# Output projection and MLP of a hybrid residual layer: seven-product first MLP layer, one block for output and MLP stages, token tiles in paired order

## The chip, the cores and the metric

One Trainium2 chip, one core. The metric is device time in microseconds (us) of the whole kernel, and the median of three runs is compared. TensorE is written PE, VectorE DVE, ScalarE ACT, GpSimd POOL, and the engine that issues the DMAs SP.

## What is computed

One layer of a streaming encoder over 1024 tokens of width 1024, all float32. What matters here are its last two lines; `mix` comes from a time mixer (RWKV-7 and stick-breaking attention), whose stages the change doesn't touch.

```
mix = merged @ w_out                                   # 1024x1024 @ 1024x1024
x   = layernorm(ALPHA * x + g1 * mix, ln1_g, ln1_b)
h   = modulate(x, sh2, sc2)                            # a second normalization, then scale and shift
ff  = square(relu(h @ w_ff1 + b_ff1)) @ w_ff2 + b_ff2  # 1024 -> 4096 -> 1024
out = layernorm(ALPHA * x + g2 * ff, ln2_g, ln2_b)
```

Each float32 matrix product is made of three bf16 products. An operand is split into a high part (its bf16 rounding, a copy on ACT) and a low part (what is left, a subtraction on POOL), and PE forms high*high + high*low + low*high.

## The kernel before

The program is a row of phases, each a block in which all five engines run their own queue of instructions in order and meet at a barrier at its end. The last three are `phase_merge` (which also begins the output product of the first token tile), `phase_out` and `phase_mlp`.

**`phase_out`** takes the 8 token tiles of 128 tokens in order. For tile t PE makes 48 matmuls of 512 columns (`out_products`, L2015). DVE adds the residual (L2346) and takes statistics; ACT normalizes (L2294); DVE applies gain (L2353) and bias (L2355), takes statistics again, ACT normalizes again into `ou_yn` (semaphore `n2`, L2282). PE transposes it (`turned_tile`, L2383) in the middle of tile t + 2, ACT scales and shifts it into `ou_hf` and copies the high part to `a_hi` (L2275), POOL makes `a_lo` (L2247). `keep` (L2335) writes the new residual to `g.x1`, a part of the buffer `z`. While the last tile is finished, PE works on the first two of the 32 tiles of 128 hidden columns (`ff_part`, L2206), with token columns that are ready.

**`phase_mlp`** takes the 32 hidden tiles in 8 groups of 4 (`GT`). `group` makes the first layer of 4 hidden tiles, 48 matmuls of 512 columns each (`gemm_rows`, L218), with ReLU on ACT (L2515), square on DVE (L2607), high part on ACT (L2519) and low part on POOL (L2552). `second` multiplies a finished group with its rows of `w_ff2` in 16 blocks of 12 matmuls (L674), which DVE adds to `g.x1` (L2619). PE makes `group(i + 1)` before `second(i)`. The weights of the first layer are loaded per hidden tile (512 KB) and split on ACT (L2437) and POOL (L2441); those of the second are loaded per group (2 MB), scaled by g2 on DVE (L2599) and split on ACT (L2524) and POOL (L2557). The last group is followed by the last normalization.

The functions that the diff touches:

Of the kernel before, what the change touches and what calls it, by code (L numbers as in the profile page):

```python
# [7 lines left out]
F32 = mybir.dt.float32  # L8
# [2201 lines left out]
def phase_out(nc, g, a):  # L2210

    with ExitStack() as es:
        sb = lambda n, s=(P, D), d=F32: es.enter_context(nc.sbuf_tensor(f"ou_{n}", list(s), d))
        names = "vec brow mm y s1 v1 sd1 r1 n1 gain bias keep s2 v2 sd2 r2 n2 turn hf hi lo tail_hf tail_hi".split()
        per_tile = {"mm": 2, "y": 2, "s1": 2, "s2": 2, "r1": 2, "r2": 2, "hf": KT}
        s = {n: nc.alloc_semaphore(f"ous_{n}") for n in names}
        s_x = [nc.alloc_semaphore(f"ous_x{u}") for u in range(2)]
        xt, y, yn = ([sb(f"{n}{u}") for u in range(2)] for n in ("x", "y", "yn"))
        hf = sb("hf", (P, KT, P))
        vec = sb("vec", (P, 3, D))  # L2220
# [23 lines left out]
        def low(eng, t):
            if inside(t):
                wait(eng, t, "hi")
                eng.tensor_tensor(g.a_lo[:, :, tok(t)], hf[:], g.a_hi[:, :, tok(t)], ALU.subtract).then_inc(s["lo"], 1)  # L2247
# [477 lines left out]
```

## Time and profile before

| | |
|---|---|
| time, median of 3 runs | 1732.8 us (1730.94 to 1733.28) |
| span of the profiled execution | 1730.9 us |
| output stage, from about 967 us | to 1076 us |
| MLP stage | from 1078 us to the end |
| PE busy | 1643.6 us, 95% of the span |
| DVE, ACT, POOL busy | 769.0, 562.3, 451.3 us |

The time of the profiled execution itself is not listed apart from its span; the median of the three runs is 1.9 us above the span. Times in the rows are in us from the span's start. A matmul of 512 columns is listed with 0.38 us, since its way through the array is counted in, but in a dense run the next one starts 0.216 us later. "[1.95 <-POOLq L88]" behind a row means that the engine was idle for 1.95 us before it, and what ended the wait.

### The profile page before, as it was taken

The numbers are of one execution on the slowest core, as the hardware profiler recorded it, in microseconds if no ns is written. First come the engines' busy times: TensorE is split into PE (matmuls) and PEld (weight loads), VectorE is DVE, ScalarE is ACT, GpSimd is POOL, SyncE is SP. The second block draws the span as 40 slices with busy tenths as digits, with TensorE's granted clock in tenths as the row PEclk, the third lists the DMA queues.
The fourth block names the chain that finished last, engine by engine and source line by source line (L and its number), as shares of the span: only waits on it lengthen the run. The fifth ranks groups of instructions, "written<-read, shape, count | busy, mean of one in ns | idle before, by whom it ended". The sixth has DMA issues, their size and how long they took to land. (4 is left out here: it accounts for less than half of the span.)

```text
span 1730.9 us, 34492 instructions
## 1 busy us (share of the span) xinstructions
PE 1643.6 (95%) x14983; PEld 857.5 (50%) x15178; DVE 769.0 (44%) x1061; ACT 562.3 (32%) x884; POOL 451.3 (26%) x236
## 2 busy tenths in 40 slices
PE   4998999998999998999999999999999999999997
PEld 2444666666545555544444455444444444444443
DVE  5597666666325455313111486433232323232338
ACT  5323544454324555411312165421211212120300
POOL 1231322222110112123422122742323333232310
PEclk9999999999999999999999999999999999999999
DMA  9851001000111200312110311420202021112002
GB/s 354 265 199 41 16 4 39 4 28 28 27 46 28 62 1 1 126 58 61 48 36 25 110 49 47 137 86 25 73 24 73 25 72 36 61 36 85 1 1 97
DMA packets 105773, 109.69 MB, mean 63 GB/s; under 512 B 2592, under 2 KB 82610, under 8 KB 105394
## 3 DMA queue, kind: packets, MB, share of 16 engines
q1 hardware_dynamic: 105648, 107.82, 19.2%
q8 instruction: 103, 1.69, 0.4%
q14 instruction: 22, 0.18, 0.0%
HBM read 101.52 MB, written 4.19 MB: 61 GB/s over the span
## 5 line engine op out<-in xcount | busy, mean ns | idle before, releaser
L218 PE MATMUL tokens_ps<-a_hi,z 128*128 128x512 bf16 x878 | 228.5, 379 | 0.9
L674 PE MATMUL ff_ps<-ff_hi,c_lo 128*128 128x512 bf16 x503 | 190.6, 379 | 0.6
L674 PE MATMUL ff_ps<-ff_hi,c_hi 128*128 128x512 bf16 x501 | 189.9, 379 | 1.4 <-DVE z L2619 0.9
L674 PE MATMUL ff_ps<-ff_lo,c_hi 128*128 128x512 bf16 x501 | 189.9, 379 | 0.6
L2619 DVE TENSOR_TENSOR z<-ff_ps,z 128x512 f32<-128x512 f32 x128 | 88.3, 690 | 205.0 <-PE ff_ps L674 204.3
L2515 ACT ACTIVATE ff_r<-tokens_ps,cols 128x1024 f32<-128x1024 f32 x30 | 33.4, 1114 | 421.4 <-PE tokens_ps L218 414.4
L2441 POOL TENSOR_TENSOR z<-z 128x1024 bf16<-128x1024 f32 x28 | 62.3, 2225 | 345.1 <-ACT z L2437 345.1
L218 PEld LDWEIGHTS tokens_ps<-a_hi,z 128*128 128x128 bf16 x896 | 87.6, 98 | 105.8
L2607 DVE TENSOR_TENSOR ff_r<-ff_r 128x1024 f32<-128x1024 f32 x32 | 41.1, 1284 | 219.2 <-ACT ff_r L2515 219.2
L218 PE MATMUL tokens_ps<-a_lo,z 128*128 128x512 bf16 x438 | 131.1, 379 | 0.5
L195 POOL TENSOR_TENSOR mg_wlo<-mg_stage,mg_whi 128x1024 bf16<-128x1024 f32 x21 | 45.6, 2175 | 149.9 <-ACT mg_whi L191 149.9
L2552 POOL TENSOR_TENSOR c_lo<-ff_r,c_hi 128x1024 bf16<-128x1024 f32 x32 | 75.9, 2371 | 29.4 <-ACT c_hi L2519 29.4
L674 PEld LDWEIGHTS ff_ps<-ff_hi,c_hi 128*128 128x128 bf16 x512 | 50.1, 98 | 61.6 <-issue 1.3
L674 PEld LDWEIGHTS ff_ps<-ff_hi,c_lo 128*128 128x128 bf16 x512 | 50.1, 98 | 60.4
L674 PEld LDWEIGHTS ff_ps<-ff_lo,c_hi 128*128 128x128 bf16 x512 | 50.1, 98 | 60.2
L808 DVE TENSOR_TENSOR_SCAN b_lo<-z,sb_ahead 128x256 f32<-128x256 f32 (+3 forms) x32 | 50.5, 1621 | 46.8 <-ACT z L925 46.8
L218 PEld LDWEIGHTS tokens_ps<-a_lo,z 128*128 128x128 bf16 x448 | 43.8, 98 | 52.9
L2557 POOL TENSOR_TENSOR ff_lo<-ff_st,ff_hi 128x1024 bf16<-128x1024 f32 x32 | 68.1, 2158 | 0.0
L2599 DVE TENSOR_TENSOR ff_st<-ff_st,z 128x1024 f32<-128x1024 f32 x32 | 67.3, 2160 | 1.7 <-DMA ff_st<-w_ff 1.7
L808 DVE TENSOR_TENSOR_SCAN b_hi<-z,sb_ahead 128x128 f32<-128x128 f32 (+3 forms) x32 | 48.3, 1551 | 43.1 <-ACT z L925 43.1
L2169 DVE TENSOR_TENSOR mg_ga<-mg_ga,mg_ps 128x1024 f32<-128x1024 f32 x7 | 8.5, 1221 | 131.6 <-PE mg_ps L218 131.6
L1648 PE MATMUL rw_front<-a_hi,z 128*128 128x512 bf16 x179 | 58.2, 387 | 3.0 <-issue 2.9
(420 smaller groups left out, 3219.2 us busy)
## 6 DMA issues: line engine op xcount, KB each, us to landing
ff_st<-w_ff SPq DMA_DIRECT2D x8, 2048.0 KB, 7.7
z<-w_ff SPq DMA_DIRECT2D x30, 512.0 KB, 4.0
ada_w<-w_ada SPq DMA_DIRECT2D x6, 2048.0 KB, 8.2
z<-w_in SPq DMA_DIRECT2D x18, 512.0 KB, 4.4
z<-w_ada SPq DMA_DIRECT2D x8, 1024.0 KB, 13.5
mg_stage<-w_in SPq DMA_DIRECT2D x16, 512.0 KB, 4.0
zs_stage<-w_in SPq DMA_DIRECT2D x8, 512.0 KB, 8.2
ada_w<-w_ada SPq DMA_DIRECT2D x4, 1024.0 KB, 13.5
```

The costliest lines, as they stand in the source:

```text
L195: pool.tensor_tensor(lo[u][:], stage[u][:], hi[u][:], ALU.subtract).then_inc(lo_ready[u], 1)
L218: last = pe.matmul(out[:, h * HALF:(h + 1) * HALF], w[:, kt, :], a[:, slot, h * HALF:(h + 1) * HALF], start=(x == 0 and y == 0), stop=(x = ...
L674: last = pe.matmul(out, a[:, slot, at], w[:, x, n], start=(x == 0 and y == 0), stop=(x == k - 1 and y == 2))
L808: dve.tensor_tensor_scan(prod[b][:, 0:nk][:, ::-1], m, masked, 1.0, ALU.mult, ALU.max).then_inc(s_scan, 1)
L1648: mm = pe.matmul(unit_bank(u)[:], w_part[:, kt, :], a_part[:, kt, h * HALF:(h + 1) * HALF], start=(x == 0), stop=(x == 3 * KT - 1))
L2441: pool.tensor_tensor(ff.lo[u], stage[u], ff.hi[u], ALU.subtract).then_inc(ff.lo_ready[u], 1)
L2515: act.activation(r[u][:], (wide if begun and t >= begun else ps1)[u][:], ACT.Relu, bias=g.cols[:, ds(gr * GT + (b1 + t), 1)]).then_inc(s_r ...
L2552: pool.tensor_tensor(g.c_lo[:, GT * par + t, :], r[u][:], g.c_hi[:, GT * par + t, :], ALU.subtract).then_inc(s_ulo[u], 1)
L2557: pool.tensor_tensor(lo2[par][:, k, :], st2[:, k, :], hi2[par][:, k, :], ALU.subtract).then_inc(s_o2, 1)
L2599: dve.tensor_tensor(st2[:, k, :], st2[:, k, :], g.g2, ALU.mult).then_inc(s_m2, 1)
L2607: dve.tensor_tensor(r[u][:], r[u][:], r[u][:], ALU.mult).then_inc(s_sq[u], 1)
L2619: dve.tensor_tensor(acc, ps2[x % 4], acc, ALU.add).then_inc(s_acc, 1)
```

## The change

`phase_out` and `phase_mlp` become one function, `phase_tail`, in one block without a barrier between the stages. All its loops are written out.

The first MLP layer takes hidden tiles in pairs (256 hidden columns) and cuts the product of a pair into 2x2 blocks: two halves of the hidden columns, two of the tokens (T0, T1), two of the summed dimension (K0, K1). Instead of eight block products it forms seven, each of 4 x 3 matmuls of 512 columns, out of sums of blocks:

- sums of activation blocks, `sums(i)`: 4 DVE instructions of 512 elements for two token tiles, then 2 high parts on ACT (`sum_high`) and 2 low parts on POOL (`sum_low`). They need a token tile of each half, so the tiles are taken in the order 0, 4, 1, 5, 2, 6, 3, 7 (`ORD`). `sums(0)` stands in the loop's turn 4, `sums(1)` in turn 6, the other two behind the loop.
- sums of weight blocks, `ff_sums`: 4 DVE instructions of 512 elements for a pair, with split copies of 512 + 1024 + 2048 elements on ACT (L2485, L2486, L2490), and as many on POOL (L2594, L2596, L2600).
- sums of products, in `pair`: DVE forms four result quarters and two intermediates (`u2`, `u3`) with 6 instructions of 512 elements that read PSUM; ReLU, square, high and low part are made per quarter (512 elements).

The first two hidden tiles stay plain (`first_part`), so 15 pairs follow, numbered n = 0 to 14. Weight set q = n + 1 is loaded as one transfer of 1 MB into one staging buffer `st1` (so a load waits until the low sums of the set before are made, `s_wsl`); the rows of `w_ff2` come in halves of a group, 1 MB each, into `st2` (a load waits for the low parts of the half before, `s_o2`). The instructions of the last tail of the kernel are the same.

```diff
-            for t in range(TT):
-                wait(pe, t - 2, "y")
-                for h in range(2):
-                    kts = [kt for kt in range(KT) if t or kt not in OUT_AHEAD]
-                    out_products(pe, g, t, slice(h * HALF, (h + 1) * HALF), kts, t > 0, True).then_inc(s["mm"], 1)
-                    if h == 0:
-                        turned_tile(t - 2)
...
+FF_ORDER = (1, 2, 6, 7, 5, 4, 3)
...
+def ff_product(pe, g, w, n, out, onto=False):
+
+    whi, wlo, bhi, blo = ff_operands(g, w)[n]
+    for kt in range(PAIRS):
+        for y, (m, b) in enumerate(((whi, bhi), (whi, blo), (wlo, bhi))):
+            last = pe.matmul(out, m[:, kt, :], b[:, kt, :], start=(kt == 0 and y == 0 and not onto), stop=(kt == PAIRS - 1 and y == 2),
+                             skip_group_check=True)
+    return last
...
+        @block.scalar
...
+                if p == NEXT_AT:
+                    act.wait_ge(s["w1"], 16)
+                    act.activation(set1.d_hi, next_st[:, K1, N1], ACT.Copy).then_inc(s["wah"], 1)
+                    act.activation(set1.a_hi, next_st[:, :, N0], ACT.Copy).then_inc(s["wah"], 1)
+                if p in SUMS_AT:
+                    sum_high(SUMS_AT[p])
+                if p == NEXT_SUMS:
+                    act.wait_ge(s["ws"], 4)
+                    act.activation(set1.s_hi, next_st, ACT.Copy).then_inc(s["wsh"], 1)
...
+            def first():
...
+                act.wait_ge(s_flo, 2)
+                second_high(0, 0, 0)
+                first_high(3, sets[1], True)
+                sums_high(3, sets[1])
+                second_high(0, 0, 1)
...
+        @block.vector
...
+            def pair(n, x, banks, free, after_c11=None, late=None):
+                of = lambda p: quads(bank(banks, x, p))
+                dve.wait_ge(s_p1, n + 1)
+                product(n, 2)
+                free(0)
+                dve.tensor_tensor(quarter(0, 0), u2, of(2), ALU.add).then_inc(s_c, 1)
...
+                product(n, 7)
+                dve.wait_ge(s_c, n * 6 + U2)
+                dve.tensor_tensor(u3, u2, of(7), ALU.add).then_inc(s_c, 1)
+                if late:
+                    late()
+                product(n, 5)
+                dve.wait_ge(s_c, n * 6 + U3)
+                free(1)
+                dve.tensor_tensor(quarter(1, 1), u3, of(5), ALU.add).then_inc(s_c, 1)
...
+            def step(i, par, last, more):
+                gr = i + 1
+                if not last:
+                    freed = lambda n: lambda k: dve.wait_ge(s_ulo, n * 4 + (k - 3))
+                    scale2(gr, 0)
+                    pair(gr * 2 - 1, 0, narrow, freed(gr * 2 - 1))
+                    scale2(gr, 1)
...
+        @block.tensor
...
+            def pair(n, x):
+                w = sets[x]
+                pe.wait_ge(s_wal, n * 2)
...
+                    if p == 5:
+                        pe.wait_ge(s_p1, n + 1)
+                    if p == 4:
+                        pe.wait_ge(s_c, n * 6 + C11)
+                    if p == 3:
+                        pe.wait_ge(s_c, n * 6 + C22)
+                    ff_product(pe, g, w, p, bank(narrow, x, p), p == 3).then_inc(s_prod, 1)
```

What the change does to the order of instructions is shown at three places. The first is ACT's queue in turn 4 of the output loop, from the first normalization of that turn's tile to its second (`yn`). Before:

```order
L2294 ACTIVATE ou_y<-ou_y,ou_rs 128x1024
L2271 ACTIVATE ou_hf<-ou_turned,ada 128x128 x8
L2275 ACTIVATE a_hi<-ou_hf 128x8x128
L150 ACTIVATE c_lo<-c_hi 128x1024
L2286 ACTIVATE ou_rs<-ou_mv,const 128x1
L2282 ACTIVATE ou_yn<-ou_y,ou_rs 128x1024
```

Of the changed kernel, where `tl_wd` and `z` are the high parts of the first weight set and `b_hi` the high parts of the activation sums:

```order
L2460 ACTIVATE tl_y<-tl_y,tl_rs 128x1024
L2430 ACTIVATE tl_pc<-ff_wide,ada 128x128 x8
L2434 ACTIVATE a_hi<-tl_pc 128x8x128
L2452 ACTIVATE tl_rs<-tl_mv,const 128x1
L2467 ACTIVATE tl_wd<-c_hi 128x512
L2468 ACTIVATE z<-c_hi 128x1024
L2439 ACTIVATE b_hi<-tl_pc 128x8x128
L2441 ACTIVATE b_hi<-tl_pc 128x8x128
L2448 ACTIVATE tl_yn<-tl_y,tl_rs 128x1024
```

Four copies now stand between the root (L2452) and the `yn` that PE's transposes wait for; the early copy L150 has moved to turn 1.

The second place is ACT's queue between the last quarter of pair 0 and the copy of pair 1's first product to `u2` (`tl_v`, L2510), in the changed kernel alone. `tl_pc` (L2495) are high parts of `w_ff2`; `tl_wd`, `z` and `tl_wsh` are those of weight set 3:

```order
L2505 ACTIVATE c_hi<-a_hi 128x512
L2495 ACTIVATE tl_pc<-tl_y 128x1024 x2
L2485 ACTIVATE tl_wd<-z 128x512
L2486 ACTIVATE z<-z 128x1024
L2490 ACTIVATE tl_wsh<-z 128x2048
L2495 ACTIVATE tl_pc<-tl_y 128x1024 x2
L2510 ACTIVATE tl_v<-tokens_ps 128x512
```

All the splitting of a weight set stands ahead of the copy that frees pair 1's PSUM bank.

The third place is DVE's queue in the second pair of a group, in the changed kernel alone. L2751 scales rows of `w_ff2`, L2772, L2777, L2781 and L2787 are sums of products, L2259 to L2264 are the sums of the next weight set in the buffer `z`:

```order
L2751 TENSOR_TENSOR tl_y<-tl_y,z 128x1024 x2
L2772 TENSOR_TENSOR a_hi<-tl_v,tokens_ps 128x2x256
L2777 TENSOR_TENSOR tl_v<-tl_v,tokens_ps 128x512
L2762 TENSOR_TENSOR a_hi<-a_hi 128x2x256
L2781 TENSOR_TENSOR tl_v<-tl_v,tokens_ps 128x512
L2259 TENSOR_TENSOR z<-z 128x4x128
L2261 TENSOR_TENSOR z<-z 128x4x128
L2263 TENSOR_TENSOR z<-z 128x4x128
L2264 TENSOR_TENSOR z<-z 128x4x128
L2787 TENSOR_TENSOR a_lo<-tl_v,tokens_ps 128x2x256
```

The weight sums stand in front of the sum (C22) for which PE's product 3 waits.

## Rows read from the trace of the kernel before

**Rows 1.** The page: busy times; shares of the chain that ended last.

```profile
PE 1643.6 (95%) x14983; PEld 857.5 (50%) x15178; DVE 769.0 (44%) x1061; ACT 562.3 (32%) x884; POOL 451.3 (26%) x236
...
PE ff_ps L674 17%; PE tokens_ps L218 17%; PE ff_ps L218 1%; DVE ff_st L2577 1%; DVE z L2594 1%; DVE z L2619 0%; DVE z L2587 0%; DVEq L2452 0%; DVE ff_rs L2589 0%; DVE ff_mv L2581 0%; POOLq L88 0%; DVEq L2593 0%; POOLq L2702 0%
```

**Rows 2.** The chain in order of time: start, us, what.

```profile
1099.66 10.74 PE tokens_ps L218 x49
```

**Rows 3.** Busy time by stretch: length, PE, PEld, DVE, ACT, POOL, PE clock, DMA.

```profile
970.00:1067.00 97.00, 96.53 (x475) 47.90 (x482) 77.96 (x121) 53.37 (x98) 19.06 (x9) 1.00 0.24 79
...
1140.00:1679.00 539.00, 536.22 (x2446) 244.16 (x2495) 157.96 (x161) 102.53 (x101) 167.67 (x76) 1.00 0.14 46
```

**Rows 4.** Timeline of PE at the end of the output stage: start, us, what, wait.

```profile
1073.28 0.23 PE L2206 MATMUL tokens_ps<-a_hi,c_lo 128*128 128x128 bf16 x1 [1.14 <-DVE a_lo L2247]
...
1078.08 0.38 PE L218 MATMUL ff_ps<-a_hi,z 128*128 128x512 bf16 x1 [1.95 <-POOLq L88]
```

**Rows 5.** Timelines of ACT and PE: second normalizations of tiles 4 to 7, transposes of 4 to 6.

```profile
1028.67 1.24 ACT L2282 ACTIVATE ou_yn<-ou_y,ou_rs 128x1024 f32<-128x1024 f32 x1 [1.12 <-DVE ou_rs L2330]
1034.68 1.04 PE L2383 MATMUL ou_turned<-const,ou_yn 128*128 128x128 f32 x8
1039.64 1.24 ACT L2282 ACTIVATE ou_yn<-ou_y,ou_rs 128x1024 f32<-128x1024 f32 x1 [1.72 <-DVE ou_rs L2330]
1045.92 1.04 PE L2383 MATMUL ou_turned<-const,ou_yn 128*128 128x128 f32 x8
1050.72 1.24 ACT L2282 ACTIVATE ou_yn<-ou_y,ou_rs 128x1024 f32<-128x1024 f32 x1 [1.73 <-DVE ou_rs L2330]
1052.02 1.09 PE L2383 MATMUL ou_turned<-const,ou_yn 128*128 128x128 f32 x8
1065.47 1.24 ACT L2282 ACTIVATE ou_yn<-ou_y,ou_rs 128x1024 f32<-128x1024 f32 x1 [1.72 <-DVE ou_rs L2330]
```

**Rows 6.** Timelines of DVE and POOL: one small DVE instruction, twice, and POOL's.

```profile
979.60 0.16 DVE L2330 SCALAR_TENSOR_TENSOR ou_rs<-ou_mv,ou_rs 128x1 f32<-128x1 f32 x1
1055.92 2.12 POOL L2247 TENSOR_TENSOR a_lo<-ou_hf,a_hi 128x1024 bf16<-128x1024 f32 x1 [5.25 <-ACT a_hi L2275]
1056.26 1.80 DVE L2330 SCALAR_TENSOR_TENSOR ou_rs<-ou_mv,ou_rs 128x1 f32<-128x1 f32 x1
```

**Rows 7.** Durations, from timelines and groups of instructions (busy us, mean ns).

```profile
961.21 0.69 DVE L2197 TENSOR_TENSOR mg_m<-mg_ga,mg_gb 128x512 f32<-128x512 f32 x1
961.93 0.63 ACT L2142 ACTIVATE b_hi<-mg_m 128x512 bf16<-128x512 f32 x1 [3.11 <-DVE mg_m L2197]
1204.77 8.50 DVE L2599 TENSOR_TENSOR ff_st<-ff_st,z 128x1024 f32<-128x1024 f32 x4
L2607 DVE TENSOR_TENSOR ff_r<-ff_r 128x1024 f32<-128x1024 f32 x32 | 41.1, 1284 | 219.2 <-ACT ff_r L2515 219.2
L2619 DVE TENSOR_TENSOR z<-ff_ps,z 128x512 f32<-128x512 f32 x128 | 88.3, 690 | 205.0 <-PE ff_ps L674 204.3
L2519 ACT ACTIVATE c_hi<-ff_r 128x1024 bf16<-128x1024 f32 x32 | 33.8, 1057 | 21.1 <-DVE ff_r L2607 21.1
L2247 POOL TENSOR_TENSOR a_lo<-ou_hf,a_hi 128x1024 bf16<-128x1024 f32 x7 | 14.9, 2124 | 89.4 <-ACT a_hi L2275 89.4
```

**Rows 8.** DMA issues: size of each, median us from issue to landing.

```profile
ff_st<-w_ff SPq DMA_DIRECT2D x8, 2048.0 KB, 7.7
z<-w_ff SPq DMA_DIRECT2D x30, 512.0 KB, 4.0
```

**Rows 9.** PE after a wait, and its clock by stretch (length, PE busy, clock).

```profile
678.34 0.63 PE L894 MATMUL tokens_ps<-a_lo,mg_whi 128*128 128x512 bf16 x1 [5.95 <-POOL mg_wlo L154]
...
676.00:677.00 1.00, 0.00 (x0) 0.64 0.00 0
...
682.00:683.00 1.00, 1.00 (x4) 0.50 0.00 0
683.00:684.00 1.00, 1.00 (x6) 0.94 0.00 0
```

More of the change, by code:

```diff
@@ L2207, in ff_part @@
     return last
-def phase_out(nc, g, a):
-    with ExitStack() as es:
[L2213 to L2220, printed above, removed]
+K0, K1 = slice(0, PAIRS), slice(PAIRS, KT)
@@ L2244, in low @@
[L2244 to L2247, printed above, removed]
+        next_st = fl(g.c_hi[:, EARLY_OUT:KT, :]).bitcast(F32).rearrange("p (k n) -> p k n", n=2 * P)
+        names = ("vec brow mm y s1 v1 sd1 r1 n1 gain bias keep s2 v2 sd2 r2 n2 turn hf hi lo "
+                 "sums xhi yhi xlo ylo w1 wah wal ws wsh wsl std").split()
+        per_tile = {"mm": 2, "y": 2, "s1": 2, "s2": 2, "r1": 2, "r2": 2, "hf": KT}
@@ new lines, in phase_tail, with wait @@
+        s_vec, s_st, s_mv, s_sd, s_rs, s_gain, s_bias, s_last, s_out = (
+            sem(n) for n in "vec st mv sd rs gain bias last out".split())
+        block = es.enter_context(nc.Block())
+        inside = lambda p: 0 <= p < TT
+        EARLY_AT, NEXT_AT, NEXT_SUMS = (1, 2), 4, 5
+        SUMS_AT = {4: 0, 6: 1}
+        LOW_AT = {5: 0, 7: 1}
+        def wait(eng, p, name, j=None):
+            k = per_tile.get(name, 1)
+            if p >= 0:
+                eng.wait_ge(s[name], p * k + (k if j is None else j))
@@ L2249, in _, with steps @@
+        def steps(first, step):
+            first()
+            for i in range(NGR):
+                step(i, i % 2, i == NGR - 1, i < NGR - 2)
         @block.sync
@@ new lines, in high, with pair @@
+            def high(par, x, n, k):
+                t, h = QUARTERS[k]
+                act.wait_ge(s_sq, n * 4 + k + 1)
+                act.activation(quads(c_at(g.c_hi, par, x, t, h)), quarter(t, h), ACT.Copy).then_inc(s_uhi, 1)
+            def pair(gr, par, x, n, early=None, late=None):
+                act.wait_ge(s_prod, n * NP + 1)
+                act.wait_ge(s_c, n * 6)
+                act.activation(u2, quads(bank(narrow, x, 1)), ACT.Copy).then_inc(s_p1, 1)
+                for k in range(4):
+                    relu(gr, x, n, k)
+                    if k == 0 and early:
+                        early()
+                    high(par, x, n, k)
+                    if k == 1 and late:
+                        late()
@@ L2572, in _ @@
+            scale(LAST, 1)
+            sums(2)
+            keep(LAST)
+            wait(dve, LAST - 1, "lo")
+            low(dve, LAST)
+            sums(3)
+            sum_low(dve, 3, 1)
             credit(dve, [s_acc])
@@ L2621, in step @@
                         norm(t, h, i * NO + x + 2)
+                    if more and 6 <= x < 10:
+                        weight_sums(gr * 2 + 3, x - 6)
                 if last:
@@ new lines, in first @@
+            def first():
+                wait(pe, LAST, "hf")
+                pe.wait_ge(s["wsl"], 1)
+                pe.wait_ge(s["xlo"], 4)
+                pe.wait_ge(s["ylo"], 4)
+                for p in FF_ORDER[2:]:
+                    if p == 5:
+                        pe.wait_ge(s_p1, 1)
+                    if p == 4:
+                        pe.wait_ge(s_c, C11)
+                    if p == 3:
+                        pe.wait_ge(s_c, C22)
+                    ff_product(pe, g, set1, p, bank(ps2, 0, p), p == 3).then_inc(s_prod, 1)
```

747 lines of the change are left out of this document (453 added, 294 removed).

## The prediction

> **What bounds the kernel now.** I read the page first: PE is busy for 95% of the span, and the chain that ended last is PE's matmuls L218 and L674 almost alone through the MLP [rows 1]. The table by stretch says it stage by stage: from 1140 to 1679 us PE works for 536.2 of 539 us, while POOL works for 168, DVE for 158 and ACT for 103 [rows 3]. There every matmul that goes away is time. The output stage is different: PE is busy for 96.5 of 97 us, but DVE for 78.0, and the work of a tile is one chain DVE, ACT, DVE, ACT, PE. So I read there how long a result lies ready before PE asks for it. The second normalization of tile 4 ends at 1028.67 + 1.24 = 1029.9 and PE transposes it at 1034.7: 4.8 us in hand. For tile 5 it is 1045.9 - 1040.9 = 5.0, for tile 6 nothing (ready at 1052.0, taken at 1052.0), and tile 7 is ready at 1066.7 [rows 5]. At the seam PE waits 1.14 and 1.95 us [rows 4].
>
> **What the change takes away.** A pair of hidden tiles costs 7 x 12 = 84 matmuls of 512 columns instead of 96. 15 pairs save 180. 49 matmuls take 10.74 us, of which 0.38 is the last one's passage, so one costs 10.36 / 48 = 0.216 us [rows 2]. Gain: 180 x 0.2158 = 38.8 us. The two waits of the seam go too, 3.1 us. Together 41.9 us: the new waits of PE must stay under this for the change to win.
>
> **What it adds, by engine.** Prices: a DVE sum of 512 elements 0.69 us, 0.73 with the step to the next dependent one; one that reads PSUM 0.69; ACT copies 0.63 (512) and 1.06 (1024); POOL 2.12 per 1024 [rows 7]. I take 2048 elements at twice the 1024: ACT 1.9, POOL 4.2. A group of two pairs then costs DVE 2 x (4 weight sums + 6 product sums + 4 squares) x 0.7 + 16 x 0.69 + 4 x 2.1 = 39 us, ACT about 25, POOL 2 x 7680 elements = 32, against 77.7 us of PE (168 + 192 matmuls). None becomes the bound by its total. What decides is the order of the queues and the following.
>
> **Two engines that exclude each other.** A DVE instruction on one column takes 0.16 us alone. At 1056.26 it takes 1.80: POOL's subtraction runs from 1055.92 to 1058.04, and the small instruction ends at 1058.06 [rows 6]. Four scalings of 1024 elements take 8.50 us amid POOL's work, 2.1 each, where a square of as many takes 1.28 on average [rows 7]. So I let a DVE instruction with two SBUF inputs wait for a running POOL subtraction to its end, and the other way round. The Trainium skill (SBUF — State Buffer, "Who interferes with whom") states just this: DVE with two SBUF inputs and a GpSimd instruction that reads SBUF block each other for a whole instruction. By that rule the trace's 1.80 us is no accident, and the sum is the one below; without it, it would be the first rival's.
>
> **The output loop.** I walked all five queues of the changed kernel in order, with these prices, from the start of the stage. The same walk over the queues of before ends its last PE instruction within half a us of the trace, so I trust it to about 1 us a stage.
> - Turn 4: `sums(0)` puts 4 x 0.73 = 2.9 us on DVE, and the bias add behind it meets POOL's subtraction (2.0). Then ACT has four more copies (0.55 + 1.0 + 1.0 + 1.0, with their overlap) before `yn`. `yn` ends 7.9 us later than at 1029.9; 4.8 were in hand: PE stalls 3.1.
> - Turn 5: `keep` waits 2.1 for POOL's `b_lo`, `ff_sums` costs 2.9 and its last part waits 2.0, ACT has the copy of 2048 (1.9) first. `yn` is 13.8 us late; minus 5.0 in hand and 3.1 already lost: 5.7.
> - Turn 6: `sums(1)` 2.9, a wait of 2.0, one of about 2 for POOL's subtraction of 2048 elements, two ACT copies 1.9. 17.7 us late, nothing in hand: 17.7 - 8.8 = 8.9.
> - Turn 7: the last tile is ready at 1084.3 instead of 1066.7. PE has two parts of 3.9 us (24 matmuls of 384 columns) in between and stalls 1.1 + 4.8.
> Sum: 23.6 us. All of this is cover that was gone: PE's transposes stand in its queue in front of the matmuls that could run.
>
> **The first pairs.** From 1084.3 PE has 19.3 us of work, in which `sums(3)` and its splits just fit. In pair 0 the product sums wait on DVE behind weight sums and the first squares, which meet POOL's 4.2 us: 5.0. Pair 1 is worst. ACT's queue holds two `w_ff2` copies, the whole splitting of weight set 3 and two more `w_ff2` copies in front of the `u2` copy. The loop through the engines: last quarter of pair 0 about 1127, copies and scalings to 1130, high parts 1.6, POOL first two `w_ff2` low parts 4.3, then 3.2, to 1137; DVE sums 2.9; ACT 1.9 + 2.0, to 1143.7; `u2` 0.7. PE's products 1, 2, 6, 7 were done at 1131.9, product 5 waits to 1144.4: 12.5. Product 4 waits for C11, which stands behind scaling the next `w_ff2` rows, whose load waits for POOL: 4.2 (set 3) + 4.3 (two low parts) to 1150.7, a load of 1 MB 5.0 (between 4.0 for 512 KB and 7.7 for 2 MB [rows 8]), scaling 2.3, C11 0.7, to 1158.8: 11.8. Pair 2: product 3 waits for C22 behind the weight sums, which wait for POOL: 6.2, and 0.6 at the second layer.
>
> **The steady groups.** The same place, with the queues recovered: 1.1 at product 3 and 0.6 at the first block of the second layer, for 5 groups 8.9. So a group saves 5.2 us of matmuls and gives 1.8 back.
>
> **The sum.** New waits 23.6 + 5.0 + 12.5 + 11.8 + 6.2 + 0.6 + 8.9 = 68.6; minus 41.9: 26.7 us slower. The clock comes on top. After a wait of 5.95 us PE's granted clock was already down to 0.5 (1.2 GHz) and stayed there until 683.06, 4.7 us after PE resumed at 678.34 [rows 9]; at half speed that is 2.35 us lost. Seven of the new waits are of 4.8 us and more: 0 to 16 us. Most of it falls before the next wait on DVE or ACT, which shrinks by as much; I take 1.5. The Trainium skill (TensorE: Matmul & The Clock Gate, "HAM oscillation — how this bites in real kernels") says the same of gaps between bursts, that each is paid again; charging each of the seven in full gives 16 instead of 1.5. Span: 1730.9 + 26.7 + 1.5 = 1759.1; the median of the runs is 1.9 above the span: **1761 us**.
>
> **Rivals.**
> - *The exclusion is weaker on these shapes* (the one on the other side). With DVE and POOL free of each other the walk gives waits of 34.6 us (the loop 9.2, pairs 1 and 2 24.4, steady groups none, 1.0 in both kernels): 33.6 - 41.9 = -8: 1725 us. It decides from under 41.9 us of waits on. Against it: the 1.80 and the 8.50 us. For it: no row shows blocks of 128 elements with gaps, as the sums have. Chance 0.05.
> - *The start of the pairs is covered better* (a load sooner, copies overlapping): the 24.3 us of pair 1 fall to about 10: 1747. Nothing in the queues speaks for it. Chance 0.06, inside my range.
> - *The clock is paid in full*: 1761 + 14.5 = 1775. Half of it is as plausible as my 1.5, since the walk has it hidden behind waits that I know to 1 us at best. Chance 0.12.
> - *POOL's large instructions cost more than linear*. At 10% more per element the walk gives 13 us more, since all chains above go through POOL: 1774. Chance 0.1.
> - *The seven products change nothing in total*: waits of just 42 us: 1733. No mechanism picks this; chance 0.02.
>
> **The numbers.** The likeliest case has 0.65 and holds 1748 to 1772. The range reaches over the clock and POOL cases to 1777 and below to 1744, and leaves out the case on the other side. What a measurement of this kernel can tell from no change is about 0.2%, 3.5 us. Slower 0.93, same 0.02, faster 0.05.
>
> **What would show it.** PE's timeline between 1030 and 1090: transposes preceded by idle time of 3, 6, 9 and 5 us, ended by ACT's `tl_yn`. One wait of some 12 us for the `u2` copy L2510 and one of some 12 us for the product sum L2772, at about 1140 to 1160. In a steady group (79.5 us from one to the next, 82.9 before) one wait of 1 us for L2787. POOL's and DVE's two-input instructions much longer than alone. Wrong I am if the transposes find their tiles ready, or if a group takes 77.7 us; then the exclusion was over-priced. A result above 1780 would mean that a queue that I took as recovered isn't, most likely POOL's.

## The result, and the profile after

The changed kernel takes 1750.6 us (median of 4, 1749.95 to 1751.0) against 1733.0 for the kernel before on the same chip: 1.0097 times as long, 95% interval 1.0082 to 1.0111. The forecast was slower with 0.93, 1761 us, range 1744 to 1777. The span of the profiled execution is 1749.0 us, 18.1 more than before.

One thing about the comparisons that follow. The code ahead of the output stage is the same in all kernels here, yet in the profiled executions that stage began anywhere from 964.95 to 969.70 us. So for effects of a few us I count from the first matmul of the output stage (L2015) to the last matmul of the kernel, start to start. That distance is 753.3 us before and 771.0 after, **17.7 us more**; nothing of the first 965 us is in it.

The page after (busy time, and shares of the chain that ended last), for [rows 1]:

```profile
PE 1621.4 (93%) x14856; PEld 847.3 (48%) x15046; DVE 904.7 (52%) x1253; ACT 615.7 (35%) x986; POOL 524.0 (30%) x288
...
PE 22%; DVE 7%; ACT 3%; POOL 3%; DMA 1%; issue 1%; DVEq 0%; POOLq 0%; ACTq 0%
```

PE lost 22.2 us of busy time, not 38.8: part of what is left ran at half the clock. What PE waited for from 965 us on (line of PE, line waited for, us in total, times, longest):

```profile
PE ff_wide L2854 <- ACT tl_yn L2448: 16.6, 4, 7.2
PE tokens_ps L2242 <- ACT tl_v L2510: 11.7, 1, 11.7
PE tokens_ps L2242 <- DVE a_hi L2772: 8.8, 1, 8.8
PE tokens_ps L2242 <- DVE a_lo L2787: 5.4, 6, 3.1
```

These are the four kinds of wait that the prediction's last part named, at their places; of the 5.0 us in pair 0 that its sum also holds, 0.15 came, and of the 0.6 at the second layer nothing. PE's timeline, the instruction behind each wait (start, us, what, wait), which answers to [rows 4] and to the transposes in [rows 5]; the first two are the transposes of tiles 4 and 5 (tiles 6 and 7 follow at 1067.35 and 1082.07, behind 7.20 and 3.38 us):

```profile
1036.09 1.09 PE L2854 MATMUL ff_wide<-const,tl_yn 128*128 128x128 f32 x8 [1.05 <-ACT tl_yn L2448]
1052.55 1.97 PE L2854 MATMUL ff_wide<-const,tl_yn 128*128 128x128 f32 x8 [5.01 <-ACT tl_yn L2448]
...
1138.55 0.61 PE L2242 MATMUL tokens_ps<-b_hi,z 128*128 128x512 bf16 x1 [11.73 <-ACT tl_v L2510]
1152.61 0.61 PE L2242 MATMUL tokens_ps<-b_hi,tl_x 128*128 128x512 bf16 x1 [8.76 <-DVE a_hi L2772]
1179.07 0.61 PE L2242 MATMUL tokens_ps<-a_hi,tl_wsh 128*128 128x512 bf16 x1 [3.06 <-DVE a_lo L2787]
1260.17 0.39 PE L2242 MATMUL tokens_ps<-a_hi,tl_wsh 128*128 128x512 bf16 x1 [0.30 <-DVE a_lo L2787]
1339.44 0.39 PE L2242 MATMUL tokens_ps<-a_hi,tl_wsh 128*128 128x512 bf16 x1 [1.16 <-DVE a_lo L2787]
```

The second column tells the clock too: a matmul behind a long wait takes 0.61 us instead of 0.39. By stretches of 1 us, PE's granted clock was 0.50 (1.2 GHz) at each wait of 3 us and more and for some us behind it. Busy time times (1 - clock), added up over 1020 to 1219 us, gives 13.6 us of lost speed: 5.5 in the loop, 5.2 in pair 1, 3.0 behind the wait in pair 2. Before it was nothing in this stretch.

Both waits of pair 1 hang on one chain. The chain that ended last, in order of time ("..." for pieces between):

```profile
1123.22 4.87 POOL tl_pc L2605 x2
...
1134.21 1.92 ACT tl_wsh L2490
...
1136.19 4.17 POOL tl_wsl L2600
1140.36 4.17 POOL tl_pc L2605 x2
1144.55 5.02 DMA tl_y<-w_ff
...
1151.95 0.61 DVE a_hi L2772
...
1156.95 5.13 POOL tl_v L2605 x2
1162.10 4.89 DMA tl_y<-w_ff
```

POOL makes low parts, the buffer comes free, the next 1 MB of `w_ff2` is loaded, and POOL again, with copies on ACT and sums and scalings on DVE between: PE is not in it. The copy L2510 that frees product 5 stands in ACT's queue behind L2490, and the sum L2772 is what product 4 waits for. And VectorE and POOL exclude each other as in [rows 6], at a new size (DVE's timeline, then POOL's, one column against 2048 elements):

```profile
1062.13 3.89 DVE L2666 SCALAR_TENSOR_TENSOR tl_rs<-tl_mv,tl_rs 128x1 f32<-128x1 f32 x1
```
```profile
1061.95 4.05 POOL L2586 TENSOR_TENSOR tl_wsl<-c_hi,tl_wsh 128x2048 bf16<-128x2048 f32 x1
```

### The profile page after: what moved, and what is told of

Its sections match the earlier page's. It is cut to its first block and busy times, and to the rows that moved or that the text cites. A ratio compares the mean times of both kernels' runs of the same rounds, so it can differ in the third digit from the quotient of the medians.

```text
span 1749.0 us, 34154 instructions
## 1 busy us (share of the span) xinstructions
PE 1621.4 (93%) x14856; PEld 847.3 (48%) x15046; DVE 904.7 (52%) x1253; ACT 615.7 (35%) x986; POOL 524.0 (30%) x288
## 5 line engine op out<-in xcount | busy, mean ns | idle before, releaser
L2834 DVE TENSOR_TENSOR z<-ff_wide,z 128x512 f32<-128x512 f32 x128 | 86.6, 687 | 151.8 <-PE ff_wide L674 151.8
L674 PE MATMUL ff_wide<-tl_pc,c_hi 128*128 128x512 bf16 x502 | 150.6, 380 | 0.7
L674 PE MATMUL ff_wide<-tl_yn,c_hi 128*128 128x512 bf16 x251 | 95.2, 379 | 1.3 <-DVE z L2834 0.9
L674 PE MATMUL ff_wide<-tl_v,c_hi 128*128 128x512 bf16 x251 | 95.1, 379 | 0.3
L674 PE MATMUL ff_wide<-tl_yn,c_lo 128*128 128x512 bf16 x251 | 95.1, 379 | 0.3
L674 PE MATMUL ff_wide<-tl_pc,c_lo 128*128 128x512 bf16 x250 | 94.8, 379 | 0.3
L674 PEld LDWEIGHTS ff_wide<-tl_pc,c_hi 128*128 128x128 bf16 x512 | 50.1, 98 | 61.5 <-DVE z L2834 1.1
L2242 PE MATMUL tokens_ps<-b_hi,z 128*128 128x512 bf16 x165 | 52.5, 391 | 11.9 <-ACT tl_v L2510 11.7
L834 PE MATMUL tokens_ps<-a_hi,z 128*128 128x512 bf16 x177 | 57.1, 388 | 0.3
L2751 DVE TENSOR_TENSOR tl_y<-tl_y,z 128x1024 f32<-128x1024 f32 x32 | 43.7, 1405 | 19.0 <-DMA tl_y<-w_ff 19.0
L2242 PE MATMUL tokens_ps<-a_hi,z 128*128 128x512 bf16 x164 | 50.2, 379 | 0.2
L2600 POOL TENSOR_TENSOR tl_wsl<-z,tl_wsh 128x2048 bf16<-128x2048 f32 x7 | 28.6, 4084 | 72.4 <-ACT tl_wsh L2490 72.4
L2762 DVE TENSOR_TENSOR a_hi<-a_hi 128x512 f32<-128x512 f32 x30 | 40.3, 1344 | 11.8 <-ACT a_hi L2500 11.8
## 6 DMA issues: line engine op xcount, KB each, us to landing
z<-w_ada SPq DMA_DIRECT2D x8, 1024.0 KB, 13.4
```

The lines of the kernel that those rows point to most:

```text
L674: last = pe.matmul(out, a[:, slot, at], w[:, x, n], start=(x == 0 and y == 0), stop=(x == k - 1 and y == 2))
L834: mm = pe.matmul(out, w_part[:, kt, :], a_part[:, kt, h * HALF:(h + 1) * HALF], start=(kt == 0 and y == 0), stop=(kt == KT - 1 and y == 2))
L2242: last = pe.matmul(out, m[:, kt, :], b[:, kt, :], start=(kt == 0 and y == 0 and not onto), stop=(kt == PAIRS - 1 and y == 2), skip_group_c ...
L2600: pool.tensor_tensor(w.s_lo, st1, w.s_hi, ALU.subtract).then_inc(s_wsl, 1)
L2751: dve.tensor_tensor(st2[:, k, :], st2[:, k, :], g.g2, ALU.mult).then_inc(s_m2, 1)
L2762: dve.tensor_tensor(quarter(*QUARTERS[k]), quarter(*QUARTERS[k]), quarter(*QUARTERS[k]), ALU.mult).then_inc(s_sq, 1)
```

## The experiments

"In the stage" is the distance defined above, 771.0 us for the changed kernel. Ratios are to the kernel before, which ran beside each kernel. The last column is the idle time ahead of the transposes in the output loop. Where it differs by about 1 us with the loop unchanged, it is tile 6 that waited 5.8 to 5.9 us instead of 7.2.

| kernel | time, us | ratio, 95% interval | in the stage | loop's waits |
|---|---|---|---|---|
| changed kernel | 1750.6 | 1.0097 (1.0082 to 1.0111) | 771.0 | 16.6 |
| e_fill | 1747.9 | 1.0075 (1.0055 to 1.0094) | 768.4 | 6.3 |
| e_fill_last | 1748.4 | 1.0091 (1.0076 to 1.0107) | 768.4 | 16.7 |
| e_u2_first | 1745.5 | 1.0070 (1.0049 to 1.0092) | 767.2 | 15.6 |
| e_start | 1728.0 | 0.9963 (0.9951 to 0.9976) | 746.4 | 15.9 |
| e_narrow_sums | 1736.6 | 1.0022 (1.0010 to 1.0035) | 757.3 | 7.5 |
| e_narrow_both | 1734.5 | 1.0012 (1.0000 to 1.0025) | 754.7 | 6.2 |
| e_low_later | 1750.5 | 1.0104 (1.0082 to 1.0127) | 771.0 | 13.4 |
| e_low_pieces | 1748.8 | 1.0096 (1.0076 to 1.0116) | 766.8 | 12.4 |
| e_copies_later | 1751.1 | 1.0106 (1.0086 to 1.0126) | 771.7 | 18.6 |
| e_extra_product | 1780.3 | 1.0272 (1.0243 to 1.0300) | 797.2 | 15.9 |
| e_start_pieces | 1726.2 | 0.9959 (0.9944 to 0.9973) | 744.0 | 12.4 |
| e_start_more | 1721.3 | 0.9941 (0.9925 to 0.9956) | 743.5 | 12.7 |

**e_fill: what the clock costs.** Six waits filled with matmuls.

```diff
+                wait(pe, p - 2, "hf")
+                for _ in range({3: 21, 4: 30, 5: 13}.get(p, 0)):
+                    pe.matmul(turned[p % 2][:, 0:HALF], g.wo[0][:, 0, 0:P], g.wo[0][:, 0, 0:HALF], ...)
                 wait(pe, p, "n2")
...
+                    fill({(1, 5): 50, (1, 4): 38, (2, 3): 13}.get((n, p), 0))
                     if p == 5:
                         pe.wait_ge(s_p1, n + 1)
```

> The changed kernel with idle TensorE time filled: matmuls of 512 columns whose result is never read stand in front of six of the waits: 21, 30 and 13 ahead of the transposes of tiles 5, 6 and 7, 50 and 38 in pair 1 ahead of products 5 and 4, 13 in pair 2 ahead of product 3. At 0.216 us each they last a little less than the waits they replace (4.5, 6.5, 2.8, 10.8, 8.2, 2.8 us), so TensorE stays busy and its clock should stay at full speed. If the half-speed work is paid in full (13.6 us is the busy time of the changed kernel times one minus the granted clock), the time falls by 11 to 14 us, to about 1738. If, as I took it, the slow matmuls lie under the wait that comes next, which then only shrinks by as much, it falls by at most 4 us, to 1747 to 1751, and the waits that are left are longer than the fillers alone would leave them.

My counting was off here: the keys 3, 4, 5 of the edit are tiles 3, 4 and 5, not 5, 6 and 7. So 21 fillers stood ahead of tile 3, where there is no wait, and 30 ahead of tile 4, where 1.05 us was to be had. The mistake shows something of its own. Counted from the stage's first matmul, TensorE transposed tile 3 4.5 us later than in the changed kernel and tile 4 9.8 us later (78.0 against 68.2); tile 6 came 0.9 later (100.3 against 99.4). A delay of 9.8 us of TensorE is nearly all absorbed within two tiles: what ends the loop's waits is not TensorE's own work.

The fillers of pairs 1 and 2 stood right. Lost speed fell from 13.6 to 4.9 us (5.2 to 1.7 in pair 1), but the stage became only 2.6 us shorter: product 4 of pair 1 started at 185.7 us (184.7 in the changed kernel), product 3 of pair 2 at 212.2 (211.1), and the gain comes behind this last long wait: to product 3 of pair 4 it took 78.4 us instead of 81.1. The stage is 1.0 us later up to that wait and 2.7 shorter behind it; the other 0.9 us is that no group had the wait of 1.16 us. The second theory holds.

**e_fill_last: where it costs.** The filler of pair 2 alone.

```diff
+                    fill({(1, 5): 0, (1, 4): 0, (2, 3): 13}.get((n, p), 0))
```

> The changed kernel with matmuls whose result is never read (13 of 512 columns, 2.8 us) in one place alone: pair 2, ahead of product 3, whose wait of 3.06 us is the last of the long ones; the five ahead of it stay bare. In the changed kernel TensorE's clock was at half speed for 5.9 us of work behind that wait. If half-speed work costs time only where no wait follows that would have taken it up, this alone gives back what filling six waits gave: 2 to 3 us less from product 3 of pair 2 to that of pair 4 (78.4 us instead of 81.1), time about 1748. If each stretch at half speed costs by itself, this one place gives at most 3 of 13.6 us and e_fill should have given 9; if the clock plays no part, 81.1 us stay.

The same 768.4 us as with six fillers, and here nearly all of it is the place named: up to pair 2 the stage is 0.2 us later, and a group with the wait of 1.16 us is there again. PE's timeline at product 3 of pairs 2 and 4; the first is at full speed now (0.39 us, 0.61 in the changed kernel):

```profile
1180.94 0.39 PE L2242 MATMUL tokens_ps<-a_hi,tl_wsh 128*128 128x512 bf16 x1 [0.27 <-DVE a_lo L2787]
1259.36 0.39 PE L2242 MATMUL tokens_ps<-a_hi,tl_wsh 128*128 128x512 bf16 x1 [0.30 <-DVE a_lo L2787]
```

78.4 us between them, against 1260.17 - 1179.07 = 81.1. Of 13.6 us of lost speed, 2.6 to 2.7 cost time: what no later wait took up. The loop shows the same without any filler. In e_start, which leaves the loop as it is, PE ran at half speed for 6.8 us behind tile 5's wait, and for 3.4 in the changed kernel. The transposes of tile 6, of the changed kernel and of e_start:

```profile
1067.35 1.97 PE L2854 MATMUL ff_wide<-const,tl_yn 128*128 128x128 f32 x8 [7.20 <-ACT tl_yn L2448]
```
```profile
1069.29 1.97 PE L2891 MATMUL ff_wide<-const,tl_yn 128*128 128x128 f32 x8 [5.90 <-ACT tl_yn L2448]
```

The wait is 1.3 us shorter, but the transposes start 99.6 us after the stage's first matmul instead of 99.4.

**e_u2_first: are pair 1's waits two or one?** ScalarE's `u2` copy of pair 1 ahead of the splitting of weight set 3.

```diff
+                if n != 1:
...
                 second_high(0, 0, 0)
+                act.wait_ge(s_prod, NP + 1)
+                act.wait_ge(s_c, 6)
+                act.activation(u2, quads(bank(narrow, 0, 1)), ACT.Copy).then_inc(s_p1, 1)
                 first_high(3, sets[1], True)
```

> The changed kernel with one instruction moved: ScalarE's copy u2 of pair 1 stands ahead of the splitting of weight set 3 instead of behind it and behind the two w_ff2 copies. If the wait of 11.7 us at product 5 is its own cause (a copy that stands too late in one queue), it vanishes and the time falls by about 11, to 1740. If the two waits of pair 1 are one chain through POOL, the DMA queue and VectorE (low parts of w_ff2 and set 3, load of the next w_ff2 rows, their scaling), product 5 no longer waits, but product 4 waits about 20 us for C11, and the time stays within 3 us of 1750.6.

```profile
PE tokens_ps L2242 <- DVE a_hi L2776: 23.0, 1, 23.0
```

One wait of 23.0 us in place of 11.7 and 8.8, and product 4 began 184.5 us after the stage's first matmul (184.7 before the edit). At the wait the edit gained 0.2 us: one chain, as the second theory has it. But the time fell by 5.1 us, outside the 3 us that I gave this theory. Of the 3.8 us by which the stage is shorter, 2.7 arose behind the 3.23 us wait of pair 2, where the clock stayed up, and 0.9 because no group had the wait of 1.16 us. Whether that is chance or something that the edit does isn't settled: the other three executions, which left no profile, took 1744.7 to 1748.8 us, all under the changed kernel's lowest, 1749.95. Busy time by stretch (length, PE, PEld, DVE, ACT, POOL, PE's clock), of the changed kernel and of this one:

```profile
1176.00:1190.00 14.00, 10.88 (x38) 4.37 (x39) 7.92 (x10) 6.98 (x8) 8.77 (x4) 0.76 0.00 1
```
```profile
1176.00:1178.00 2.00, 1.43 (x7) 0.70 (x8) 1.21 (x3) 0.72 (x1) 0.00 (x0) 1.00 0.03 8
1178.00:1180.00 2.00, 2.00 (x11) 0.87 (x9) 0.60 (x1) 1.97 (x3) 1.26 (x2) 1.00 0.00 0
```

**e_start: the order of the start.** Weight set 3 is split inside pair 1, the second half of the first `w_ff2` rows inside pair 2, and the `w_ff2` rows of group 1 and sets 4 and 5 beside `second(0)`. ScalarE's part (DVE's and POOL's follow it):

```diff
                 second_high(0, 0, 0)
-                first_high(3, sets[1], True)
-                sums_high(3, sets[1])
-                second_high(0, 0, 1)
...
+                if i == 0:
+                    pair(1, 1, 0, 1, lambda: first_high(3, sets[1], True), lambda: sums_high(3, sets[1]))
+                    pair(1, 1, 1, 2, lambda: second_high(0, 0, 1))
+                    second_high(1, 1, 0)
+                    first_high(4, sets[0], True)
+                    sums_high(4, sets[0])
+                    second_high(1, 1, 1)
+                    first_high(5, sets[1], True)
+                    sums_high(5, sets[1])
+                    return
```

> The changed kernel with the start of the pairs in another order on ScalarE, VectorE and POOL: weight set 3 is split inside pair 1, the second half of the first w_ff2 rows inside pair 2, and the w_ff2 rows of the next group and weight sets 4 and 5 beside the first second-layer stage. PE's queue and all arithmetic stay. If the two long waits of pair 1 and the one of pair 2 (11.7, 8.8, 3.1 us) come from the order of these queues, at most one wait of 3 to 6 us is left there and the time falls by 18 to 24 us, to 1727 to 1732, under the kernel before. If the work itself is too much for this stretch, the waits come back at the first second-layer stage or at pair 3, and the time stays above 1743.

24.5 us less in the stage (23.7 of them up to product 3 of pair 4, 0.9 from the missing wait of 1.16 us), and 0.4% faster than the kernel before. What PE waits for from 965 us on:

```profile
PE ff_wide L2891 <- ACT tl_yn L2448: 15.9, 4, 5.9
PE tokens_ps L2242 <- DVE a_lo L2809: 5.8, 6, 4.2
PE ff_wide L674 <- POOL tl_pc L2612: 1.8, 1, 1.8
```

The two long waits are gone; a wait of 4.2 us at product 3 of pair 1 and one of 1.8 us at the second layer stand in their place. The work was never too much for the stretch; its order was wrong.

**e_narrow_sums, e_narrow_both: the loop.** The block sums of the first four tiles on 1 column (VectorE's part; these two kernels leave parts of the sums out of the result):

```diff
...
+                if i < 2:
+                    of1, of2 = of1[:, :, 0:1], of2[:, :, 0:1]
```

> The changed kernel with the block sums of the first four tiles (on VectorE, ScalarE and POOL, inside the output loop) on 1 column instead of 128 per block: all instructions and waits stay, their sizes don't, and these parts of the activation sums are left out of the result. If the sums make the waits ahead of the transposes, they fall from 16.6 us to 5 to 9 (turn 4 none, turn 5 about 1, turns 6 and 7 about 3.5 each, which the next weights' copies and sums make), and the time falls by 9 to 14 us, to 1737 to 1742. If it is the weights' copies and sums alone, the time falls by less than 4 us.

13.7 us less in the stage; the waits of tiles 4 and 5 are gone, those of tiles 6 and 7 are 3.03 and 4.45. Tile 7's transposes come 12.0 us sooner, and product 3 of pair 2 is still 12.0 sooner; the rest arises behind it. So the activation sums make about half of the 22.8 us that the loop loses (in waits and lost speed). With the weight sums narrow too:

> e_narrow_sums with VectorE's four sums of the first pair's weights in the output loop (ff_sums) on 2 columns of each block instead of 128 as well; these weight sums and the activation sums of four tiles are then left out of the result, while the copies and low parts of the weights stay. Whether VectorE's own 2.9 us of ff_sums or ScalarE's and POOL's copies and splits for the weights make the 7.5 us of waits left in e_narrow_sums: by VectorE, they fall to about 2 at tile 4 and 5 and the time is 3 to 4 us under e_narrow_sums, 1733; by ScalarE and POOL, the waits stay at 7 and the time too, 1736 to 1737.

The waits fell from 7.5 to 6.2 us only, and pair 1 and 2 began 1 us sooner. The rest of the 2.7 us comes behind pair 2, where the clock stayed up this time. So VectorE's own weight sums are worth about 1 us; what makes the remaining 6.2 us wasn't taken apart. Nor did any run move the transposes in PE's queue, behind matmuls that could have run, which the prediction gave as the reason why a late tile stalls PE.

**e_low_later, e_low_pieces: the exclusion.** POOL's subtraction of 2048 elements behind the loop, or in four pieces where it was (the edit shown).

```diff
-                    pool.tensor_tensor(set1.s_lo, next_st, set1.s_hi, ALU.subtract).then_inc(s["wsl"], 1)
+                    for c in range(4):
+                        cc = slice(c * KT // 4, (c + 1) * KT // 4)
+                        i = pool.tensor_tensor(set1.s_lo[:, cc], next_st[:, cc], set1.s_hi[:, cc], ALU.subtract)
+                    i.then_inc(s["wsl"], 1)
```

> The changed kernel with POOL's subtraction of 2048 elements (low part of the first pair's weight sums) moved out of the output loop, behind its last b_lo. In the changed kernel VectorE's one-column instruction L2666 took 3.89 us beside this subtraction. If the two engines exclude each other for whole instructions, that instruction falls to 0.16 us here and some VectorE instruction beside the moved subtraction takes up to 4 us. For the time: by the order of the queues the subtraction is now late for the first pair (TensorE needs it, and POOL's splitting of the next weights stands behind it), and the time rises by 2 to 6 us, to about 1755; if the 3.7 us in the loop were a loss of their own, it falls by 3 to 4, to about 1747.

> The changed kernel with the same subtraction of 2048 elements cut into four of 512, in the same place. Exclusion for whole instructions: VectorE's one-column instruction beside it falls from 3.89 to at most 1.2 us. If this stall sets the wait ahead of tile 4's transposes, the time falls by 2 to 3 us; if the chain over ScalarE's copies of the sums and POOL's splits is as long as the one over VectorE, the time falls by 0.5 us, which is within the uncertainty.

(What this text and that of e_start_pieces call tile 4 is tile 6: the stall at 1062.13 stands in VectorE's turn 6.)

Moved away, the small DVE instruction takes 0.16 us, and another DVE instruction with two SBUF inputs, 1.23 us in the changed kernel, takes 5.09 beside the moved one (DVE's timeline, then POOL's):

```profile
1060.45 0.16 DVE L2665 SCALAR_TENSOR_TENSOR tl_rs<-tl_mv,tl_rs 128x1 f32<-128x1 f32 x1
...
1084.57 5.09 DVE L2352 TENSOR_TENSOR a_lo<-tl_pc,a_hi 128x1024 bf16<-128x1024 f32 x1 [2.02 <-ACT a_hi L2434]
```
```profile
1084.50 4.07 POOL L2588 TENSOR_TENSOR tl_wsl<-c_hi,tl_wsh 128x2048 bf16<-128x2048 f32 x1
```

The stall moved with its cause, and so did the loss: tile 6's transposes came 2.4 us sooner, and product 3 of pair 0 waited 2.73 us for VectorE's sum (0.15 before). At product 3 of pair 2 the stage is 1.3 us behind the changed kernel, and gets that back behind this wait, where the clock was at half speed for 3.4 us instead of 6.8. I had expected 1755 or 1747; it is 1750.5, since the loop gained what I had not given it. In four pieces (DVE, then POOL):

```profile
1062.78 0.99 DVE L2669 SCALAR_TENSOR_TENSOR tl_rs<-tl_mv,tl_rs 128x1 f32<-128x1 f32 x1
1063.69 0.67 DVE L2697 SCALAR_TENSOR_TENSOR tl_y<-tl_x,tokens_ps 128x512 f32<-128x512 f32 x1
```
```profile
1062.61 4.50 POOL L2588 TENSOR_TENSOR tl_wsl<-c_hi,tl_wsh 128x512 bf16<-128x512 f32 x4
```

DVE waits for the first piece alone. Then an instruction with one input in PSUM runs its usual 0.67 us beside POOL's other pieces. Up to pair 2 the stage is 2.1 us ahead; the median is 1.8 us lower, but the ratio (1.0096 for 1.0097) doesn't show it, the interval is as wide as the gain.

**e_copies_later: turn 4's queue.** ScalarE's copies behind the second normalization in turns 4 to 6.

```diff
...
                 if p == NEXT_AT:
+                    second(p)
                     act.wait_ge(s["w1"], 16)
...
                 if p == NEXT_SUMS:
+                    second(p)
```

> The changed kernel with ScalarE's copies for the next weights and the block sums behind the second normalization of the tile, no longer ahead of it, in turns 4, 5 and 6. Queue-order theory (my prediction gave turn 4's stall to the four copies ahead of tl_yn): turn 4's wait of 1.05 us goes, and if the copies are what the transposes wait for, the loop's waits fall from 16.6 to under 10 and the time by 5 to 8 us. Chain theory (VectorE and POOL need what the copies make, so that it comes later now): the wait of turn 5 grows to 7 to 9 us, the sum of the loop's waits rises by 2 to 6, and the time is 0 to 4 us above 1750.6.

```profile
1052.55 1.97 PE L2859 MATMUL ff_wide<-const,tl_yn 128*128 128x128 f32 x8 [6.73 <-ACT tl_yn L2448]
1068.60 1.97 PE L2859 MATMUL ff_wide<-const,tl_yn 128*128 128x128 f32 x8 [7.28 <-ACT tl_yn L2448]
```

Tile 4's wait went, and tiles 5, 6 and 7 wait 6.73, 7.28 and 4.58 us (5.01, 7.20, 3.38 before the edit): 18.6 us and 1.7 more for a low part, against 16.6. ScalarE then stood idle for 8.44 us until VectorE had the next statistics. No gain: tile 4's wait was the copies' doing, as the first theory says, but the sum is that of the chain theory. (The copy L150 that stood in turn 4 before stands in turn 2 in the changed kernel, not in turn 1: it starts at 1006.46 us.)

**e_extra_product: is PE the bound in the steady groups?**

```diff
+                    if p == 1 and n >= 3:
+                        ff_product(pe, g, w, p, bank(narrow, x, p))
```

> The changed kernel with product 1 computed twice in each of the 12 pairs from the third on (the first result is overwritten): 144 matmuls more, 31.1 us by 0.216 us each. If TensorE is the bound in the steady groups, as I took it, the time rises by 29 to 31 us, to about 1781, and the waits of 0.3 us at product 3 hardly change. If something else (the transfers, VectorE and POOL excluding each other) set a good part of the 78.4 us of a group, it rises by clearly less than 25.

29.8 us more in the median. In the stage it is 26.2 more, because this execution kept its clock behind pair 2 (2.7 us) and had no group with a wait of 1.16 us (0.9). Busy time from 1190 to 1720 us:

```profile
1190.00:1720.00 530.00, 529.43 (x2446) 238.22 (x2445) 247.05 (x299) 131.72 (x167) 200.17 (x108) 1.00 0.14 48
```

The steady waits of 0.30 us, which I had expected to stay, are gone too, and 144 matmuls cost 29.8 of 31.1 us. TensorE is the bound there. A group of the changed kernel takes 78.4 us, and its 360 matmuls need 77.7 of them, so a product not made is worth nearly what it takes.

**e_start_pieces, e_start_more: versions that beat both kernels.** The second adds five moves of order to the first. Two of them, the copies of turn 4 ahead of the pieces and the split of the last block sums ahead of the copies of weight set 2:

```diff
+                if p == NEXT_AT:
+                    act.wait_ge(s["w1"], 16)
+                    act.activation(set1.d_hi, next_st[:, K1, N1], ACT.Copy).then_inc(s["wah"], 1)
+                    act.activation(set1.a_hi, next_st[:, :, N0], ACT.Copy).then_inc(s["wah"], 1)
                 piece(p - 2 if p < LAST else p - 1)
...
-                first_high(2, sets[0], False)
                 sum_high(3)
+                first_high(2, sets[0], False)
```

> The reordered start of the pairs (e_start) together with POOL's subtraction of 2048 elements in four pieces (e_low_pieces). If the gains are each their own, as the places of the waits say (tile 4's transposes came 2.3 us earlier in e_low_pieces, pairs 1 and 2 win 23 us in e_start), the time is 1 to 3 us under e_start, about 1726. If the 2.3 us were an accident of one execution, it is that of e_start within its uncertainty, 1728.

> e_start_pieces with five more moves of order, none of arithmetic: the load of the next pair's weights one turn earlier and ScalarE's copies of them ahead of the pieces in turn 4; the split of the last block sums ahead of the copies and splits of weight set 2 on ScalarE and on POOL; in pair 1 the sums of weight set 3 behind C22 instead of ahead of it; the second half of the first w_ff2 rows ahead of pair 2's quarters. Walk of the queues: 5 us under e_start_pieces, about 1721 (turn 4's wait gone, the first pair 1.6 us less, the wait at pair 1's product 3 replaced by one of about the same size in pair 2, the one at the first second-layer stage gone). If each wait only moves to the next place, it is within 1.5 us of e_start_pieces.

e_start_pieces is 2.5 us shorter than e_start in the stage, where tile 6's transposes come 2.5 us sooner (2.4 in e_low_pieces): in the traces the gains add up. The medians differ by 1.7 us, and the intervals of the two ratios overlap. e_start_more has the best median, 1721.3, just what its walk gave, but the profiled execution has it by luck: its stage began at 964.95 us, that of e_start_pieces at 969.46, and the two stages differ by 0.5 us (743.5 and 744.0). That the five moves gain more than this isn't shown; its six times lie in two groups, 1720.1 to 1721.5 and 1726.3 to 1726.5, and only one of them left a profile. Its waits moved, as the second theory said:

```profile
PE ff_wide L2897 <- ACT tl_yn L2449: 12.7, 3, 6.3
PE tokens_ps L2242 <- DVE a_hi L2823: 2.6, 1, 2.6
PE tokens_ps L2242 <- DVE a_lo L2813: 2.4, 5, 1.2
PE ff_wide L2242 <- DVE a_lo L2813: 2.4, 1, 2.4
```

Turn 4's wait is in tile 5's now (6.33 us), and pair 0 waits 2.40 us that it didn't before. Either kernel is faster than the one before by 0.4 to 0.6%, with the seven products kept.

## Why the prediction was right, and where its sizes were off

The direction and the reason hold. The change takes away 38.8 us of matmuls, and e_extra_product, where added ones cost nearly their full time, says that they are worth nearly that; it adds waits in the loop and in the first pairs that cost more. Place by place, the idle time of PE, the lost speed beside it and 0.16 us for each wait (a wait is counted from the modelled end of the matmul ahead, 0.38 us instead of 0.216), against the prediction:

| place | predicted | idle | lost speed | sum |
|---|---|---|---|---|
| output loop | 23.6 | 16.6 | 5.5 | 22.8 |
| pair 0 | 5.0 | 0.2 | 0 | 0.3 |
| pair 1 | 12.5 + 11.8 = 24.3 | 11.7 + 8.8 | 5.2 | 26.0 |
| pair 2 | 6.2 + 0.6 | 3.1 | 3.0 | 6.2 |
| steady groups | 8.9 | 2.4 | 0 | 3.2 |
| sum, with 1.5 for the clock | 70.1 | 42.8 | 13.6 | 58.5 |

The two waits of the seam were 3.1 us and, with 0.16 for each, 3.4. 58.5 - 38.8 - 3.4 = 16.3, against 17.7 measured in the stage; 1.4 us stay unassigned. (The steady groups' 8.9 was 5 times 1.1 + 0.6, rounded up.)

- *The loop, pairs 1 and 2:* within 2 us each, as sums of idle time and slow work. The chain that holds PE up is ScalarE's, VectorE's, POOL's and the transfers', so it ends when it ends; a PE at half speed merely waits less. That is why waits behind slow work came out below the forecast (product 4 8.8 for 11.8, product 3 of pair 2 3.1 for 6.2) and the places did not. e_u2_first showed the two waits of pair 1 to be one chain, to 0.2 us, and e_start that it is an affair of order: 24.5 us, more than the whole loss of the change. Turn 4's wait, 1.05 us for 3.1, has another cause, for the clock was still full there: VectorE came first, its bias add (L2711) took 1.22 us from 1028.42 and POOL's subtraction 3.07 from 1028.56, where I had the bias add wait 2.0.
- *The clock:* mis-sized in the text's small term, 1.5, by little: the fillers give back 2.7 us, in the table a part of pair 2. Lost speed was 13.6, yet the rival that has it paid in full is out.
- *Pair 0:* the first mis-sized term, 5.0 for 0.2. Tile 7's transposes came at 1082.07 instead of 1084.3, which is 2.2 of it. The rest, about 3 us, must lie in my walk of VectorE's and POOL's work for the first pair; no run took it apart.
- *Steady groups:* the second, 8.9 for 3.2 in waits. Two waits of 1.1 and 0.6 us are no bigger than the error that I gave the walk, 1 us a stage, and I took them five times. Four of the five groups gave 0.30 at product 3, one 1.16, and none a wait at the second layer. A group took 78.4 us, not the 79.5 forecast, and that is nearer the 77.7 that the prediction called a sign of an over-priced exclusion. What was too high in the walk there, the exclusion's price or another, wasn't tested.
- The two make 10.4 us together, and the forecast's 28.2 (26.7 + 1.5) is 10.5 above the 17.7 measured. That the two fill the distance is in part luck: the loop, pair 1, pair 2, the clock and the seam are off by 0.8, 1.7, 0.6, 1.5 and 0.3 us, 1.4 us are unassigned, and all these cancel. The time, 1750.6, lies near the lower end of the likeliest case, 1748 to 1772.
- *Exclusion of VectorE and POOL:* it holds at each new shape, 3.89 us beside 4.05, 5.09 beside 4.07, 0.16 with the neighbour gone. The rival without it (1725 us) is out. By the Trainium skill (SBUF — State Buffer, "Who interferes with whom") a VectorE instruction with at most one SBUF input doesn't contend; the 0.67 us of L2697 beside POOL's pieces agrees.
- *Start of the pairs covered better* (1747): not so in this kernel, and the price of that cover was 24 us, not the 14 that I gave it. *POOL's large instructions more than linear* (1774): no, 2048 elements took 4.05 to 4.08 us, a little under twice the 2.12.

Where the expected 41.9 us went, then: 23 into the output loop, 26 into pair 1, 6 into pair 2. What makes the loop's 23 is settled in part: 12.0 us hang on the block sums of the first four tiles, and of the 11 that are left about 1 on VectorE's weight sums. The rest wasn't taken apart.

## What to carry to other kernels

When work is taken from the bounding engine and put on the others, look first at the stretches in which they have no lead, the start of a pipeline above all: there the order of their queues decided 24 us, with the same instructions. Before pricing a wait, find the chain that ends it; moving one late instruction to the front gained 0.2 us of 11.7, moving the chain's work left 4.2 and 1.8 us of 23.6. Add up slow clock and idle time as one term up to the next wait, and a term below the error of the estimate should not be multiplied by the number of groups.

## What was not expected of the hardware

A wait of about 3 us may or may not lower the clock. Behind product 3 of pair 2 PE's clock fell after waits of 3.06 us (0.76 on the mean over 1176 to 1190 us) and 3.93 (0.88), but stayed at 1.00 after 3.23, 3.29, 3.34 and 3.64 in four other executions; it also fell after 3.86 in e_low_later and 4.15 in e_narrow_sums. Where it fell, the way to product 3 of pair 4 took 1.4 to 2.7 us more than the 78.4 us without. And the same code ahead of the output stage took from 964.95 to 969.70 us in the profiled executions, which is more than several of the effects looked for here.
